# A 16-matmul gates unit with both weight parts in one stationary tile, behind the first X unit

## What is computed

```python
proj = u @ w_in
xm, z, o_pre, i_pre, f_pre = jnp.split(
    proj, [M_INNER, 2 * M_INNER, 3 * M_INNER, 3 * M_INNER + M_HEADS], axis=-1)
...
log_i = jnp.transpose((i_pre + b_i).astype(jnp.float32), (0, 2, 1))
log_f = jnp.transpose(jax.nn.log_sigmoid((f_pre + b_f).astype(jnp.float32)), (0, 2, 1))
```

## Time and profile before

| what | value |
|---|---|
| median of three runs | 1779.04 us |
| lowest, highest | 1778.79, 1779.22 us |
| the profiled execution: its own time | 1780.06 us |
| the profiled execution: span of its instructions | 1778.2 us |
| granted TensorE clock, mean | 0.997 of full speed |
| TensorE matmul (PE) | 1766.3 us busy, 9474 matmuls |
| weight load (PEld) | 1506.6 us busy |
| DVE / ACT / POOL | 1223.2 / 850.6 / 266.0 us busy |

### The profile page before, as it was taken

The page is one execution under the profiler, slowest core; times in us unless marked ns, Lnnn a source line. Parts: engine busy times, 40 slices in busy tenths (PEclk is TensorE's granted clock), DMA queues, the critical chain, the costliest instruction groups (busy, mean ns, idle before and its releaser), DMA issues.

```text
span 1778.2 us, 24809 instructions
## 1 busy us (share of the span) xinstructions
PE 1766.3 (99%) x9474; PEld 1506.6 (85%) x9474; DVE 1223.2 (69%) x1473; ACT 850.6 (48%) x1197; POOL 266.0 (15%) x270
## 2 busy tenths in 40 slices
PE   9999999999999999999999999999999999999997
PEld 7899989888777788889989888888888888888886
DVE  6778657543777655678747567887586677868984
ACT  5445335424555544345425465453353444466663
POOL 3011010211000002001101330200101101213333
PEclk9999999999999999999999999999999999999998
DMA  6345342344221225345434223232222222223243
GB/s 239 109 133 174 121 132 71 105 148 142 87 70 59 83 95 174 98 121 176 143 105 121 72 96 112 79 99 85 95 83 89 95 83 83 94 96 106 96 131 107
DMA packets 56151, 195.94 MB, mean 110 GB/s; under 512 B 6680, under 2 KB 8856, under 8 KB 56048
## 3 DMA queue, kind: packets, MB, share of 16 engines
q1 hardware_dynamic: 39408, 135.55, 23.2%
q0 software_dynamic: 16208, 58.55, 11.0%
q10 hardware_dynamic: 432, 0.40, 0.1%
HBM read 190.26 MB, written 2.11 MB: 108 GB/s over the span
## 4 chain that ended last, share of the span: by engine, by line
PE 99%; DMA 0%; DVE 0%; ACT 0%; POOL 0%; POOLq 0%; issue 0%; ACTq 0%; DVEq 0%
PE banks L639 24%; PE banks L641 23%; PE banks L640 23%; PE banks L758 6%; PE banks L757 6%; PE banks L756 6%; PE banks L855 1%; PE banks L874 1%; PE banks L898 1%; PE banks L1033 1%; PE banks L1035 1%; PE banks L1034 1%; PE banks L1061 0%; PE banks L1059 0%; PE banks L1060 0%; PE banks L818 0%
## 5 line engine op out<-in xcount | busy, mean ns | idle before, releaser
L2070 DVE TENSOR_TENSOR w_lo<-w_raw,w_hi 128x1024 fp32r<-128x1024 f32 x249 | 316.9, 1273 | 305.3 <-ACT w_hi L1331 304.2
L1331 ACT ACTIVATE w_hi<-w_raw 128x1024 fp32r<-128x1024 f32 x249 | 263.3, 1058 | 379.2 <-PE banks L641 337.6
L639 PE MATMUL banks<-u_hi,w_hi 128*128 128x512 f32 x1016 | 400.6, 394 | 0.6 <-DVE u_lo L2087 0.6
L641 PE MATMUL banks<-u_hi,w_lo 128*128 128x512 f32 x1016 | 395.8, 390 | 0.0
L640 PE MATMUL banks<-u_lo,w_hi 128*128 128x512 f32 x1016 | 395.4, 389 | 0.0
L639 PEld LDWEIGHTS banks<-u_hi,w_hi 128*128 128x128 f32 x1016 | 190.8, 188 | 42.2 <-issue 2.2
L641 PEld LDWEIGHTS banks<-u_hi,w_lo 128*128 128x128 f32 x1016 | 190.7, 188 | 40.7
L640 PEld LDWEIGHTS banks<-u_lo,w_hi 128*128 128x128 f32 x1016 | 190.9, 188 | 38.7 <-issue 0.5
L758 PE MATMUL banks<-xs_hi,w_lo 128*128 128x256 f32 x512 | 144.9, 283 | 0.0
L757 PE MATMUL banks<-xs_lo,w_hi 128*128 128x256 f32 x512 | 144.9, 283 | 0.0
L756 PE MATMUL banks<-xs_hi,w_hi 128*128 128x256 f32 x512 | 144.9, 283 | 0.0
(11 more groups left out here) (390 smaller groups left out, 3434.9 us busy)
## 6 DMA issues: line engine op xcount, KB each, us to landing
w_raw<-weights SPq DMA_DIRECT2D x251, 512.0 KB, 3.5
m<-matrices POOLq DMA_DIRECT2D x48, 512.0 KB, 4.5
mx<-matrices POOLq DMA_DIRECT2D x32, 512.0 KB, 5.0
m_even<-matrices POOLq DMA_DIRECT2D x8, 512.0 KB, 7.0
sq<-matrices POOLq DMA_DIRECT2D x8, 512.0 KB, 6.9
bias<-neighbour_bias POOLq DMA_DIRECT2D x8, 384.0 KB, 5.1
v_win<-v_a POOLq DMA_DIRECT2D x16, 128.0 KB, 4.7
out_t<-x SPq DMA_DIRECT2D x16, 128.0 KB, 1.8
```

The costliest lines, as they stand in the source:

```text
L639: nc.tensor.matmul(o, wh, hi, start=start and k == 0, stop=False)
L641: ins = nc.tensor.matmul(o, wl, hi, start=False, stop=stop and k == len(pairs) - 1)
L1331: nc.scalar.activation(w_hi[:, n.slot, :], w_raw[:, n.slot, :], ACT.Copy).then_inc(hi_ready, 1)
L2070: nc.vector.tensor_tensor(w_lo[:, n.slot, :], w_raw[:, n.slot, :], w_hi[:, n.slot, :].bitcast(F32), ALU.subtract)\
```

## The change

Three things are changed, all around the unit G.

- **One stationary tile.** `w_hi` and `w_lo` become two views of one tensor `w_split`, with the high and low part of a slot side by side. The gates' unit is laid out in DRAM so that for input chunk k the 64 high columns and the 64 low columns together are every 16th number of the slot's 2048. This strided tile of 128 columns is the stationary operand of two matmuls (with `u_hi` and with `u_lo`), 16 matmuls for the unit. The low weights' results come out in rows 64 to 67 and 96 to 99 of a bank of its own, bank 7, and DVE scales these rows too and adds them.
- **Order of units.** X(0,0) comes before G in the stream. X(0,0)'s chunks 0 to 6 wait for `u_lo` chunk by chunk; two chunks of G stand ahead of the wait for chunk 7.
- **Statistics.** They stand behind chunk 0 of X(0,1), ahead of its chunk 1.

G keeps its place 0 in `M_LINEAR`, so all other units keep their banks, and X(0,2), whose `before` is G, waits for what position 0 waited for.

```diff
+GATES_BANK = 7
...
-    units = [("G",)] + [("X", 0, c) for c in range(4)] + [("O", 0, 0), ("O", 0, 1), ("O", 0, 3)]
+    units = [("X", 0, 0), ("G",)] + [("X", 0, c) for c in range(1, 4)] + [("O", 0, 0), ("O", 0, 1), ("O", 0, 3)]
...
+M_LINEAR = [("G",)] + [o for o in M_LINEAR if o[0] != "G"]
...
-        w_hi = sb("w_hi", [P, 2, UB * P], F32R)
-        w_lo = sb("w_lo", [P, 2, UB * P], F32R)
+        w_split = sb("w_split", [P, 2, 2, UB * P], F32R)
+        w_hi, w_lo = w_split[:, :, 0, :], w_split[:, :, 1, :]
...
                     before = M_LINEAR[i - 3]
-                    if before[0] in "QK":
+                    if before[0] == "G":
+                        pe.wait_ge(bank_read, G_GATES - 2 + 3)
+                    elif before[0] in "QK":
...
-            unit_ready(unit_of("G"))
-            linear_free("G")
+            def gates_chunk(k):
+
+                both = w_split[:, unit_of("G").slot, :, :].rearrange("p a b -> p (a b)")[:, k::2 * UB]
+                nc.tensor.matmul(bank[GATES_BANK][:, :], both, u_hi[:, k, :], start=k == 0, stop=False)
+                ins = nc.tensor.matmul(bank[GATES_BANK][:, :], both, u_lo[:, k, :], start=False, stop=k == DC - 1)
+                if k == DC - 1:
+                    ins.then_inc(unit_used, 1)
+
+            unit_ready(unit_of("X", 0, 0))
+            linear_free("X", 0, 0)
             for k in range(DC - 1):
                 pe.wait_ge(u_lo_ready, DC * 3 + k + 1)
-                linear_chunk(k, "G")
-            unit_ready(unit_of("X", 0, 0))
-            linear_free("X", 0, 0)
-            linear_chunk(0, "X", 0, 0)
+                linear_chunk(k, "X", 0, 0)
+            unit_ready(unit_of("G"))
+            for k in range(2):
+                gates_chunk(k)
             pe.wait_ge(u_lo_ready, DC * 3 + DC)
-            linear_chunk(DC - 1, "G")
-            for k in range(1, DC):
-                if k == 6:
+            linear_chunk(DC - 1, "X", 0, 0)
+            for k in range(2, DC):
+                gates_chunk(k)
+            unit_ready(unit_of("X", 0, 1))
+            linear_free("X", 0, 1)
+            for k in range(DC):
+                if k == 1:
...
-                linear_chunk(k, "X", 0, 0)
-            for c in range(1, 4):
+                linear_chunk(k, "X", 0, 1)
+            for c in range(2, 4):
                 linear("X", 0, c)
...
-            gb = bank[linear_bank("G")]
+            gb = bank[GATES_BANK]
+            i_low, f_low = m_row, e_row
+            step(nc.vector.tensor_tensor(i_low[:, :], gb[64:68, :], rstd[64:68, :], ALU.mult))
+            step(nc.vector.tensor_tensor(f_low[:, :], gb[96:100, :], rstd[96:100, :], ALU.mult))
             step(nc.vector.tensor_tensor(i_row[:, :], gb[0:4, :], rstd[0:4, :], ALU.mult))
             evict(nc.vector.tensor_tensor(f_row[:, :], gb[32:36, :], rstd[32:36, :], ALU.mult), "G")
             lo("X", 0, 2)
             dve.wait_ge(bank_read, evicted("G"))
-            step(nc.vector.tensor_scalar(f_row[:, :], f_row[:, :], vecs[0:4, V_BIF + 1:V_BIF + 2], None, ALU.add))
             step.wait()
-            step(nc.vector.tensor_scalar(i_row[:, :], i_row[:, :], vecs[0:4, V_BIF:V_BIF + 1], None, ALU.add))
+            step(nc.vector.scalar_tensor_tensor(f_row[:, :], f_row[:, :], vecs[0:4, V_BIF + 1:V_BIF + 2], f_low[:, :],
+                                                ALU.add, ALU.add))
+            step.wait()
+            step(nc.vector.scalar_tensor_tensor(i_row[:, :], i_row[:, :], vecs[0:4, V_BIF:V_BIF + 1], i_low[:, :],
+                                                ALU.add, ALU.add))
...
         if kind == "G":
-            columns(gates, 0)
+            unit = np.zeros((P, UB * P // 16, 16), np.float32)
+            unit[:, :, :DC] = gates[:, :UB * P // 16].reshape(DC, P, UB * P // 16).transpose(1, 2, 0)
+            units.append(unit.reshape(P, UB * P))
```

## The result

The changed kernel takes 1787.7 us (median of six runs, 1786.95 to 1788.83), the kernel before 1778.99 us beside it (1778.79 to 1779.52): a ratio of 1.0049, with a 95% interval of 1.0037 to 1.0061. The forecast was 1784.0 us with a range of 1782.0 to 1787.5; the median lies 0.2 us above the range. The direction was right, 3.7 us of the size were missing.

What follows compares the result with a forecast made beforehand. It took the number of matmuls in PE's stream and its standstills as the bound; -1.81 + 3.54 + 0.01 + 3.33 = 5.07 us, 4.97 laid out in time, on the median 1779.04 gave 1784.0 us, range 1782.0 to 1787.5.

Steps and rivals of the forecast that it cites:

- Part 1: In the PE stream, eight matmuls fewer at 0.2267 us each: 1.81 us of work go.
- Part 2: At the hand-over, X(0,0), now first, waits for the add that empties the last feed-forward column's bank: 3.54 us lost.
- Part 3: Ahead of X(0,1), the wait for its weights is hidden with no cover left: 0.01 us.
- Part 4: Ahead of X(0,2), PE waits 3.33 us for weights behind DVE's longer eviction chain: 9.70 us with 6.54 us of cover.
- The strided tile: In the gates' weight loads, taken as free; as a rival, four times the price adds 2.9 us: 1786.9 us, chance 0.08.
- The text's own bracket: For the strided load: twice the column price, 0.20 us, still hides beneath a matmul; four times, 0.41 us, sets the distance.
- rival 1: Clock falls to half in a stall at the hand-over: +1.7 us each, 1785.7 for one, 1787.4 for two; chance 0.20.
- The argument for it: At the kernel's sparse end, the clock fell to 1.2 GHz with more matmuls in the records than a stall has.
- the restart: On PE after a wait ends, the time until the stream effectively runs again: 0.17 us.

Runs made afterwards that it cites:

- e9: Changed kernel with banks 0 and 1 exchanged, weight splits of several units moved earlier, and q's low part ahead of the gates' second scan: 1777.87 us, ratio 0.9993.
- e1: Changed kernel with banks 0 and 1 exchanged, so X(0,0) takes the free bank and X(0,2) that of the last feed-forward column: 1783.98 us, ratio 1.0028.
- e8: Changed kernel run once more, nothing edited, for a second profile: 1788.44 us (one run).
- e11: Changed kernel with six filler matmuls ahead of each of two waits, X(0,0)'s for its bank and X(0,2)'s for its weights: 1784.43 us, ratio 1.0031.
- e7: Changed kernel with twelve filler matmuls ahead of each of two waits, X(0,0)'s for its bank and X(0,2)'s for its weights: 1784.29 us, ratio 1.0029.
- e2: Changed kernel with the weight splits of X(0,2), X(0,3) and O(0,0) moved earlier on ACT and DVE, the bank wait left: 1784.9 us, ratio 1.0030.
- e5: Changed kernel with twelve filler matmuls ahead of X(0,2)'s wait for its weights alone: 1785.78 us, ratio 1.0034.

## Why the prediction was off

**Part 1 held** (the eight matmuls). Up to X(0,2) stand 64 matmuls in place of 72, beside the five of the statistics, and `e9`, where no stall is left at the hand-over, keeps 1.2 us of the 1.81.

**Part 2 held** (X(0,0) waits for its bank). In the first profile the second matmul of X(0,0) starts at 1037.97, so the stream effectively begins at 1037.74, where it could have begun at 1034.19: 3.55 us, against 3.54. The bank is shown as the cause by `e1`.

**Part 3 held** (the weights of X(0,1)). There is no gap ahead of X(0,1), and little to spare: weights ready at 1045.54 + 1.23 = 1046.77, and the matmul at 1047.03.

**Part 4 held** (the weights of X(0,2)). From the start of the statistics to the end of the weights it took 1057.43 - 1047.71 = 9.72 us, against 9.70; the evictions were 0.71 apart, as taken. Between the starts of the last matmul of X(0,1) and the first of X(0,2) lie 3.44 us (1055.62 to 1059.06 in `e8`), less 0.23, plus 0.11 for the slow second one at full clock (`e11`): 3.32, against 3.33. That the sum without the clock agrees with `e7` is thus not luck: its parts agree one by one.

**The strided tile** was taken as free and costs 0.15 us. The text's own bracket, that a column of twice the price is hidden, was nearly right: 1.6 times is hidden but for 0.009 us a matmul.

**The failed step is rival 1, the clock.** It was given 0.20 and left out of the sum. It is what happens in most cases: of seven stalls of 3.0 to 3.3 us in profiled executions (two in each profile of the changed kernel, one each in `e1`, `e2`, `e5`), five brought half clock. The argument against it, "dense work up to and behind each stall", was no protection: ahead of both stalls the matmuls followed each other at 0.227 us. The argument for it, was stronger than it was taken for; the clock came down there between gaps well under 1 us, and the step from "seen at the end of the kernel" to "to be expected behind 3 us of nothing" was not made. The rule named beside it (the Trainium skill, TensorE: Matmul & The Clock Gate, Part 1: idleness takes the engine to half rate) is borne out by the windows above. The price given to the clock was also off: 1.7 us for a fall, where the falls at the first stall cost 1.5 and 1.6 and those at the second 2.7 and 2.8. The guess was that the low level lasts as long as the stall. It lasted 3.4 us with stalls of 3.31 us and 6.8 us with stalls of 3.05, so the length isn't that of the stall. Nor does it start at a fixed place: it came between 0.9 us ahead of the restart and 1.0 us behind it. What did hold is the half: 1.57 us lost in 3.4 us of half clock with matmuls (`e8`), 2.79 in 6.1 (first profile). What sets the length, and why two stalls so alike differ, stays open.

The account from the median of before: 1779.04 - 1.81 + 3.55 + 3.32 + 0.15 - 0.10 = 1784.15, and `e7` has 1784.29. With the second fall alone it is 1786.9, with both 1788.5; the six runs lie from 1786.95, which is the one profiled with the second fall alone, to 1788.83. The four of 1787.4 to 1787.8 between them fit neither sum well, and no profile shows which falls they had.

## What to carry to other kernels

- A unit that moves to the front of a stream takes its waits with it. Ask of each: what covered it in the old place? Here a bank that came free 1.4 us ahead of need became a 3.5 us stall, for a gain of 1.8 us.
- A stall of TensorE of some 3 us mostly costs more than its length: in five of seven cases another 1.5 to 2.8 us were lost at half clock. If a stall can't be removed, idle matmuls in it are worth trying; twelve in each of two stalls gave back 3.4 us here.
- Removing a stall brings work forward on the engines beside it. Read the next place where they are full, here Q(0)'s weights some 30 us on, before counting the gain.

## What had not been expected of the hardware

- The same program, with the same 3.31 us stall, kept full clock in one execution and fell to half in another. A change that adds such a stall also widens the spread: 2.7 us in `e1` and 3.3 in `e2` (nine runs each), where 29 runs of the kernel before spread over 1.3 us.
- A stationary tile of 128 columns with a step of 16 bytes or more loads in 0.30 to 0.33 us in place of 0.19, and beneath a matmul of 512 columns nearly all of that is hidden.
- The first matmul behind a stall is followed at 0.31 to 0.34 us at full clock, 0.08 to 0.11 more than the usual distance. That is part of what the prediction called the restart.
- Half clock can set in before a stall is over, or after it: 0.8 and 0.9 us ahead of the restart at the second stall, 1.0 us behind it in `e5`.
